# One 1024-column instruction per engine for the split of a weight block, and a ring counted in whole blocks

## The chip, the cores and the metric

The kernel runs on one core of a Trainium2 chip. The metric is the time of one execution in microseconds (us). A profiled execution, taken by the hardware profiler, gives the rows that are read here. TensorE (PE in the profile; PEld is its loading of stationary weights) multiplies matrices, VectorE (DVE) and ScalarE (ACT) work elementwise, GpSimd is POOL, and SyncE (SP) issues the DMA transfers.

## The reference, cut to what matters

The kernel computes an encoder of two layers over 256 tokens of width 1024, in float32. Each layer is

```
h = rms_norm(x);  proj = h @ w_in                      # 50 blocks of 128 output columns
gates = sigmoid(h @ w_gate + b_gate)                   # 24 blocks
o_lru, o_diff, o_swa = mixers(proj)                    # recurrence, two attentions
x += (sum_b gates_b * (o_b @ w_branch_b)) @ w_out      # 24 blocks, then 8 blocks
h = rms_norm(x);  q = h @ w_q                          # 16 blocks
routing weights G from top_k(q @ subkeys)              # 16 experts for each of 8 heads
x += (G * gelu(h @ u.T)) @ v                           # 128 blocks, then 128 blocks
```

A final norm follows. The last product is computed densely: all 16384 experts' activations, weighed by G, which is zero for those that weren't chosen.

## The kernel before

**Blocks.** All weights come from HBM as one stream of blocks of 128 x 1024 float32, 106 blocks for the first part of a layer and 272 for the second, 756 in all. They are of two kinds. In an up block (w_in, w_gate, w_branch, w_q, u) the weights are the stationary operand: 8 pieces of 128 columns, each with three matmuls over 256 tokens, 24 matmuls that add up in one PSUM bank. In a down block (w_out, v) the weights are the moving operand: two halves of 512 columns, two token tiles and three matmuls each, 12 matmuls that add up over all blocks.

**The split.** TensorE multiplies in a shorter format (fp32r), so each operand is split into a high part and the rest, and a product takes three matmuls (hi x hi, hi x lo, lo x hi). For weights, ScalarE writes w_hi (split_hi, L275: a Copy from raw into the fp32r tile) and VectorE writes w_lo = raw - w_hi (split_half, L282). Both work by halves of 512 columns, k = 0 and k = 1; split_lo is the two halves one after the other. For down blocks the activations are split as well: ScalarE a_hi (L366), then VectorE a_lo (L370), each 128x256.

**The ring.** raw holds two pairs of blocks; SyncE loads a pair with one DMA (load_pairs, L259) as soon as the pair that lay there is fully split. w_hi and w_lo hold four halves, which is two blocks. Three semaphores count halves: w_hi_done (ScalarE to VectorE), w_parts (VectorE to TensorE and to SyncE) and w_used (TensorE to ScalarE, one increment behind the last matmul of each half). So ScalarE may write half k of block c when TensorE has used half k of block c-2, and TensorE may start on half k of c when its w_lo is there.

**Order of the work around it.** Each engine runs its own program; in a loop body for up blocks ScalarE does split_hi of block c+1, waits until TensorE has used all of block c, and reads the result of c out of PSUM (L503, L516, L1021, L1042). In the branch blocks VectorE does this reading (L808, L811, L832). In down blocks ScalarE does split_hi and then a_hi, VectorE split_lo and then a_lo, and down_block waits for a_lo of its block as well.

VectorE has other work in many stages: small chains for the recurrence's constants, the convolution, the scan, the lists of top_k. There the halves are put between dependent instructions by hand: half(0), an instruction, half(1), the next, and so on. In the candidate loop (L1176 on), one round handles one list and four U blocks: its last calls are half(5), an is_equal (L1198), half(6), a multiply (L1202), half(7) and a reduction (L1205), the last three over 128x800. The one-hot stage between the up and the down blocks of the second part (L1245 to L1307) uses no weights.

Of the kernel before, what the change touches and what calls it, by code (L numbers as in the profile page):

```python
# [128 lines left out]
def trunk(nc, stream, vecs, cst, rel_bias, bucket_onehot, lam_consts, final_g, diff_lambda, sinks,  # L129
# [6 lines left out]
    with top:  # L136
# [115 lines left out]
        def load_pairs(sp, layer, part_pair, first, end):  # L252

            base = layer * LAYER_PAIRS + part_pair

            def load(p, slot):

                sp.wait_ge(w_parts, p * 4 + 4)
                sp.dma_start(raw[:, slot, :, :], stream[bass.ds(base + p, 1)].rearrange("o b p c -> p (o b) c")).then_inc(raw_in[slot], 16)  # L259
            twos = (end - first) // 2  # L260
            with sp.Fori(0, twos) as n:
                load(n * 2 + first, first % 2)
                load(n * 2 + (first + 1), (first + 1) % 2)
            if (end - first) % 2:
                load(end - 1, (end - 1) % 2)

        def split_hi(act, blk, ring):

            slot, sub = ring // 2, ring % 2
            if sub == 0:  # L270

                act.wait_ge(raw_in[slot], blk * 4 + (16 - 4 * ring))
            for k in range(2):
                act.wait_ge(w_used, blk * 2 + (k + 1))
                act.activation(w_hi[:, (ring % 2) * 2 + k, :], raw[:, slot, sub, 512 * k:512 * k + 512], ACT.Copy).then_inc(w_hi_done, 1)  # L275

        def split_half(dve, blk, ring, k):

            slot, sub = ring // 2, ring % 2
            q = (ring % 2) * 2 + k  # L280
            dve.wait_ge(w_hi_done, blk * 2 + (k + 1))
            dve.tensor_tensor(w_lo[:, q, :], raw[:, slot, sub, 512 * k:512 * k + 512], w_hi[:, q, :].bitcast(F32), ALU.subtract).then_inc(w_parts, 1)  # L282

        def split_lo(dve, blk, ring):

            for k in range(2):
                split_half(dve, blk, ring, k)
# [97 lines left out]
        with nc.Fori(0, DEPTH) as layer:  # L385

            with ExitStack() as part:
# [33 lines left out]
                with nc.Block() as block:  # L421
                    @block.sync
                    def _(sp):
                        sp.sem_inc(w_parts, 8)
# [64 lines left out]
                    def _(act):  # L489
# [24 lines left out]
                        def read_proj(blk, ring):  # L514
                            act.wait_ge(w_used, blk * 2 + 6)
                            act.activation(one(proj[:, bass.ds(blk, 1), :]), bank[ring % 2][:, 0:SEQ], ACT.Copy).then_inc(up_read, 1)  # L516
# [119 lines left out]
                    def _(dve):  # L636
# [165 lines left out]
                        for k in range(16):  # L802
# [3 lines left out]
                            dve.wait_ge(w_used, blk * 2 + 6)  # L806
# [17 lines left out]
                        with dve.Fori(0, 2) as n:  # L824
                            ch.enter(n, 8)
                            for i in range(4):
# [4 lines left out]
                                dve.wait_ge(w_used, blk * 2 + 6)  # L831
# [13 lines left out]
                        add_to_x(dve, bank[2:6], 2 * MIX_BLOCKS + 4)  # L845

                    @block.tensor
                    def _(pe):
                        pe.sem_inc(w_used, 4)
# [113 lines left out]
            with ExitStack() as part:  # L963
# [34 lines left out]
                with nc.Block() as block:  # L998
                    @block.sync
                    def _(sp):  # L1000
                        sp.sem_inc(w_parts, 8)
# [9 lines left out]
                    def _(act):  # L1011
# [5 lines left out]
                        def read_up(dst, func):  # L1017
                            def body(k, blk, ring, n, i):
                                split_hi(act, blk + 1, (ring + 1) % 4)
                                act.wait_ge(w_used, blk * 2 + 6)  # L1020
                                act.activation(one(dst(k)), bank[ring % 2][:, 0:SEQ], func).then_inc(up_read, 1)  # L1021
# [18 lines left out]
                        def read_gelu(k, ring):  # L1040
                            act.wait_ge(w_used, (k + B_U) * 2 + 6)
# [78 lines left out]
                    def _(dve):  # L1120
# [151 lines left out]
                        add_to_x(dve, bank[4:8], 2 * PEER_BLOCKS + 4)  # L1272

                    @block.tensor
                    def _(pe):
                        pe.sem_inc(w_used, 4)
# [132 lines left out]
```

## Time and profile before

| | |
|---|---|
| time, median of 3 runs (lowest to highest) | 2850.52 us (2848.39 to 2858.77) |
| span of the profiled execution | 2819.8 us |
| mean granted TensorE clock | 0.967 |
| TensorE busy | 2601.8 us, 92% |
| VectorE busy | 1788.4 us, 63% |
| ScalarE busy | 1554.7 us, 55% |
| DMA, share of 16 engines | 42.5% |

The span runs from the first to the last instruction of the profiled execution; the time of a run also holds what lies around it. The busy share of TensorE is high because its matmuls overlap in the drawing: each is drawn from its start to its modelled end, and the next starts before that. Distances from start to start show its pace. A wait in a row is the idle time of an engine just before an instruction, with the instruction that ended it.

### The profile page before, as it was taken

What the parts mean: (1) busy time and instruction counts of PE and PEld (TensorE: products, weight loads), DVE (VectorE), ACT (ScalarE), POOL (GpSimd) and SP (SyncE); (2) the same over time, 40 slices, a digit from 0 to 9 for tenths busy, and PEclk for the clock granted to TensorE, in tenths of its full rate; (3) what the DMA queues carried; (4) which work ended last, traced back from release to release, by engine and by line L of the source; (5) the groups of instructions that cost most, each with busy time, mean ns of one, the idle gap of its engine ahead of it and who ended that gap; (6) DMA issues with size and microseconds to landing.
All of it is one profiled execution on the core that took longest, in us unless ns stands there. A gap on an engine that the chain in (4) does not pass through costs nothing. (4 is left out here: it accounts for less than half of the span.)

```text
span 2819.8 us, 57502 instructions
## 1 busy us (share of the span) xinstructions
PE 2601.8 (92%) x17506; PEld 2377.8 (84%) x17506; DVE 1788.4 (63%) x4078; ACT 1554.7 (55%) x3535; POOL 53.4 (2%) x115
## 2 busy tenths in 40 slices
PE   5999999899999769999989999979999997799997
PEld 5998788899999758888779987869999996688886
DVE  3655566377775796666546545654877748966665
ACT  3565344465555785555455643535555558755554
POOL 0000100000000000000000011000000000000000
PEclk9999999899999999999989979989999999999999
DMA  5444123445554205555444431334555541055553
GB/s 181 164 164 156 31 86 135 165 164 179 186 185 164 74 1 193 193 193 193 149 160 164 166 115 28 106 124 163 183 179 186 185 164 45 30 194 193 193 193 141
DMA packets 116256, 413.83 MB, mean 147 GB/s; under 512 B 8104, under 2 KB 18144, under 8 KB 115936
## 3 DMA queue, kind: packets, MB, share of 16 engines
q1 hardware_dynamic: 116192, 413.06, 42.5%
q8 instruction: 30, 0.49, 0.1%
q14 instruction: 34, 0.28, 0.0%
HBM read 411.43 MB, written 4.23 MB: 147 GB/s over the span
## 5 line engine op out<-in xcount | busy, mean ns | idle before, releaser
L282 DVE TENSOR_TENSOR w_lo<-raw,w_hi 128x512 fp32r<-128x512 f32 x1512 | 1023.2, 689 | 751.6 <-ACT w_hi L275 736.3
L275 ACT ACTIVATE w_hi<-raw 128x512 fp32r<-128x512 f32 x1512 | 902.2, 627 | 389.5 <-PE bank L315 307.9
L298 PE MATMUL bank<-h_hi,w_hi 128*128 128x256 f32 x3488 | 998.5, 286 | 28.4 <-DVE w_lo L282 28.4
L299 PE MATMUL bank<-h_lo,w_hi 128*128 128x256 f32 x3488 | 993.0, 285 | 0.0
L300 PE MATMUL bank<-h_hi,w_lo 128*128 128x256 f32 x3488 | 992.6, 285 | 0.0
L298 PEld LDWEIGHTS bank<-h_hi,w_hi 128*128 128x128 f32 x3488 | 675.8, 194 | 33.2 <-DVE w_lo L282 32.9
L299 PEld LDWEIGHTS bank<-h_lo,w_hi 128*128 128x128 f32 x3488 | 676.1, 194 | 0.4
L300 PEld LDWEIGHTS bank<-h_hi,w_lo 128*128 128x128 f32 x3488 | 675.7, 194 | 0.0
L313 PE MATMUL bank<-w_hi,a_hi 128*128 128x512 f32 x1088 | 425.1, 391 | 8.3 <-issue 5.0
L314 PE MATMUL bank<-w_lo,a_hi 128*128 128x512 f32 x1088 | 424.6, 390 | 0.0
L315 PE MATMUL bank<-w_hi,a_lo 128*128 128x512 f32 x1088 | 424.4, 390 | 0.0
L1042 ACT ACTIVATE A<-bank 128x256 f32 (+1 forms) x256 | 98.0, 383 | 341.5 <-PE bank L300 341.5
L313 PEld LDWEIGHTS bank<-w_hi,a_hi 128*128 128x128 f32 x1088 | 205.0, 188 | 51.9 <-issue 5.3
L315 PEld LDWEIGHTS bank<-w_hi,a_lo 128*128 128x128 f32 x1088 | 205.0, 188 | 42.7
L314 PEld LDWEIGHTS bank<-w_lo,a_hi 128*128 128x128 f32 x1088 | 205.1, 189 | 42.3
L1307 PE MATMUL bank<-hot 128*128 128x128 f32 x1024 | 149.0, 289 | 74.7 <-DVE hot L1249 68.7
L1307 PEld LDWEIGHTS bank<-hot 128*128 128x128 f32 x1024 | 125.4, 193 | 98.3 <-issue 85.6
L298 PE MATMUL bank<-o_hi,w_hi 128*128 128x256 f32 x384 | 111.5, 290 | 4.2 <-DVE o_lo L798 4.2
L1099 ACT ACTIVATE hot<-picks,picks_t 128x128 f32<-128x128 f32 x256 | 112.2, 485 | 4.1 <-PE bank L1307 1.7
L299 PE MATMUL bank<-o_lo,w_hi 128*128 128x256 f32 x384 | 110.6, 288 | 0.0
L300 PE MATMUL bank<-o_hi,w_lo 128*128 128x256 f32 x384 | 110.6, 288 | 0.0
L370 DVE TENSOR_TENSOR a_lo<-A,a_hi 128x256 fp32r<-128x256 f32 x256 | 106.8, 417 | 1.0 <-ACT a_hi L366 1.0
(197 smaller groups left out, 2236.7 us busy)
## 6 DMA issues: line engine op xcount, KB each, us to landing
raw<-stream SPq DMA_DIRECT2D x378, 1024.0 KB, 4.8
hank<-rel_hankel SPq DMA_DIRECT2D x16, 256.0 KB, 2.7
rel_hankel<-rel_line SPq DMA_DIRECT2D x1, 3072.0 KB
hank<-rel_hankel SPq DMA_DIRECT2D x16, 128.0 KB, 2.1
A<-subkeys SPq DMA_DIRECT2D x2, 1024.0 KB, 5.0
x<-x_in SPq DMA_DIRECT2D x1, 1024.0 KB, 5.3
qk<-lru_w SPq DMA_DIRECT2D x2, 512.0 KB, 9.1
out<-xr SPq DMA_DIRECT2D x2, 512.0 KB
```

The source lines that it names most:

```text
L275: act.activation(w_hi[:, (ring % 2) * 2 + k, :], raw[:, slot, sub, 512 * k:512 * k + 512], ACT.Copy).then_inc(w_hi_done, 1)
L282: dve.tensor_tensor(w_lo[:, q, :], raw[:, slot, sub, 512 * k:512 * k + 512], w_hi[:, q, :].bitcast(F32), ALU.subtract).then_inc(w_parts, 1)
L298: pe.matmul(ps, hi, rhs_hi(4 * k + c), start=first, stop=False)
L299: pe.matmul(ps, hi, rhs_lo(4 * k + c), start=False, stop=False)
L300: ins = pe.matmul(ps, lo, rhs_hi(4 * k + c), start=False, stop=last)
L313: pe.matmul(ps, hi, w_hi[:, q, :], start=first, stop=False)
L314: pe.matmul(ps, hi, w_lo[:, q, :], start=False, stop=False)
L315: ins = pe.matmul(ps, lo, w_hi[:, q, :], start=False, stop=last)
L370: dve.tensor_tensor(a_lo[:, a, :], src(k), a_hi[:, a, :].bitcast(F32), ALU.subtract).then_inc(a_parts, 1)
L1042: act.activation(one(A[:, bass.ds(k, 1), :]), bank[ring % 2][:, 0:SEQ], ACT.Gelu_apprx_tanh).then_inc(up_read, 1)
L1099: ins = act.activation(hot[:, s, 1, k, :], dist[:, s, k - 1, :], ACT.Relu, scale=picks_t[:, 3, bass.ds(t, 1)], bias=picks_t[:, 2, bass.ds( ...
L1307: ins = pe.matmul(bank[2 + s][:, P * k:P * k + P], hot[:, s, 0, k, :], hot[:, s, 1, k, :], start=True, stop=True)
```

## The change

Each engine splits a whole block with one instruction of 1024 columns. The semaphores w_hi_done, w_parts and w_used count blocks, with starting values of half the former ones, and all waits on them are rewritten. ScalarE waits before the whole block's w_hi until block c-2 is used entirely; TensorE waits once, ahead of a block's first matmul, for the whole w_lo, and increments w_used once, behind its last. split_half keeps its name and its places: with k = 0 it does the whole block, with k = 1 it does nothing. The size of the ring, the loads, the matmuls and all other instructions stay.

```diff
-                sp.wait_ge(w_parts, p * 4 + 4)
+                sp.wait_ge(w_parts, p * 2 + 2)
...
-            for k in range(2):
-                act.wait_ge(w_used, blk * 2 + (k + 1))
-                act.activation(w_hi[:, (ring % 2) * 2 + k, :], raw[:, slot, sub, 512 * k:512 * k + 512], ACT.Copy).then_inc(w_hi_done, 1)
+            act.wait_ge(w_used, blk + 1)
+            act.activation(whole_of(w_hi, ring), raw[:, slot, sub, :], ACT.Copy).then_inc(w_hi_done, 1)
+
+        def whole_of(parts, ring):
+
+            return parts[:, (ring % 2) * 2:(ring % 2) * 2 + 2, :].rearrange("p k c -> p (k c)")
 
         def split_half(dve, blk, ring, k):
 
+            if k:
+                return
             slot, sub = ring // 2, ring % 2
-            q = (ring % 2) * 2 + k
-            dve.wait_ge(w_hi_done, blk * 2 + (k + 1))
-            dve.tensor_tensor(w_lo[:, q, :], raw[:, slot, sub, 512 * k:512 * k + 512], w_hi[:, q, :].bitcast(F32), ALU.subtract).then_inc(w_parts, 1)
+            dve.wait_ge(w_hi_done, blk + 1)
+            dve.tensor_tensor(whole_of(w_lo, ring), raw[:, slot, sub, :], whole_of(w_hi, ring).bitcast(F32), ALU.subtract).then_inc(w_parts, 1)
...
         def up_block(pe, blk, ring, n_up, ps, rhs_hi, rhs_lo):
 
             pe.wait_ge(up_read, n_up + 1)
+            pe.wait_ge(w_parts, blk + 5)
             for k in range(2):
                 q = (ring % 2) * 2 + k
-                pe.wait_ge(w_parts, blk * 2 + (k + 9))
...
-                ins.then_inc(w_used, 1)
+            ins.then_inc(w_used, 1)
...
         def down_block(pe, blk, ring, k_blk, acc, first, last):
 
             pe.wait_ge(a_parts, k_blk + 1)
             a = ring % 2
+            pe.wait_ge(w_parts, blk + 5)
             for k in range(2):
                 q = (ring % 2) * 2 + k
-                pe.wait_ge(w_parts, blk * 2 + (k + 9))
...
-                ins.then_inc(w_used, 1)
+            ins.then_inc(w_used, 1)
...
-                                act.wait_ge(w_used, blk * 2 + 6)
+                                act.wait_ge(w_used, blk + 3)
```

## Rows read from the trace of the kernel before

**Rows 1.** The page's groups: line, engine, operation | busy, mean ns | idle before, releaser

```profile
L282 DVE TENSOR_TENSOR w_lo<-raw,w_hi 128x512 fp32r<-128x512 f32 x1512 | 1023.2, 689 | 751.6 <-ACT w_hi L275 736.3
L275 ACT ACTIVATE w_hi<-raw 128x512 fp32r<-128x512 f32 x1512 | 902.2, 627 | 389.5 <-PE bank L315 307.9
```

**Rows 2.** The waits of the whole span: who <- whom: us in total, times, longest

```profile
DVE w_lo L282 <- ACT w_hi L275: 736.3, 898, 12.1
...
PEld bank L298 <- DVE w_lo L282: 32.9, 17, 4.1
```

**Rows 3.** Windows in up blocks, down blocks, one-hot stage: us, busy (instructions), PEclk, DMA

```profile
575.00:860.00 285.00, 284.55 (x2372) 284.35 (x2371) 222.29 (x652) 153.92 (x373) 0.00 (x0) 1.00 0.52 182
1060.00:1400.00 340.00, 340.00 (x1502) 281.63 (x1501) 214.78 (x375) 195.97 (x374) 0.00 (x0) 1.00 0.55 189
...
1000.00:1040.00 40.00, 26.64 (x185) 22.37 (x186) 40.00 (x95) 35.87 (x95) 0.00 (x0) 1.00 0.00 0
```

**Rows 4.** Timeline in the down blocks: start, us, engine, line, operation [idle <- releaser]

```profile
1201.51 0.39 PE L315 MATMUL bank<-w_hi,a_lo 128*128 128x512 f32 x1
...
1201.93 0.63 ACT L275 ACTIVATE w_hi<-raw 128x512 fp32r<-128x512 f32 x1 [0.73 <-PE bank L315]
...
1202.60 0.69 DVE L282 TENSOR_TENSOR w_lo<-raw,w_hi 128x512 fp32r<-128x512 f32 x1 [0.67 <-ACT w_hi L275]
...
1203.21 0.42 DVE L370 TENSOR_TENSOR a_lo<-A,a_hi 128x256 fp32r<-128x256 f32 x1
...
1204.46 0.39 PE L313 MATMUL bank<-w_hi,a_hi 128*128 128x512 f32 x1
```

**Rows 5.** Timeline in the U blocks, candidate loop

```profile
761.16 0.38 ACT L1042 ACTIVATE A<-bank 128x256 f32 x1 [1.46 <-PE bank L300]
...
761.44 1.14 ACT L275 ACTIVATE w_hi<-raw 128x512 fp32r<-128x512 f32 x2
...
763.62 0.28 PE L300 MATMUL bank<-h_hi,w_lo 128*128 128x256 f32 x1
...
763.74 0.28 PE L298 MATMUL bank<-h_hi,w_hi 128*128 128x256 f32 x1
...
764.22 0.98 DVE L1205 TENSOR_REDUCE A<-A 128x800 f32 x1
```

**Rows 6.** Timeline in the gate blocks

```profile
251.94 1.14 ACT L275 ACTIVATE w_hi<-raw 128x512 fp32r<-128x512 f32 x2
...
254.05 0.28 PE L298 MATMUL bank<-h_hi,w_hi 128*128 128x256 f32 x1
```

**Rows 7.** Longer instructions: ns min/median/max by source line; one group by shape

```profile
L325 ACT ACTIVATE mix<-x x4: 1039/1048/1057, 15.8 to 1416.4; 128x1024 f32<-128x1024 f32 x4
...
L337 ACT ACTIVATE mix<-x,rstd x2: 1149/1150/1151, 19.0 to 1418.6; 128x1024 f32<-128x1024 f32 x2
...
L1343 DVE SCALAR_TENSOR_TENSOR xr<-x,rstd,g_all x2: 1279/1282/1285, 2814.1 to 2815.3; 128x1024 f32<-128x1024 f32 x2
...
L1202 DVE TENSOR_TENSOR A<-A 128x800 f32<-128x800 f32 x32 | 31.5, 984 | 0.0
```

**Rows 8.** Timeline where TensorE stands waiting for a split

```profile
139.44 1.15 ACT L275 ACTIVATE w_hi<-raw 128x512 fp32r<-128x512 f32 x2 [0.20 <-ACT warm L320]
...
140.10 1.29 DVE L282 TENSOR_TENSOR w_lo<-raw,w_hi 128x512 fp32r<-128x512 f32 x2 [4.28 <-ACT w_hi L275]
...
140.85 0.39 PE L298 MATMUL bank<-h_hi,w_hi 128*128 128x256 f32 x1 [0.78 <-DVE w_lo L282]
```

**Rows 9.** Timeline and window after a longer pause of TensorE

```profile
864.38 0.46 PE L298 MATMUL bank<-h_hi,w_hi 128*128 128x256 f32 x1 [2.55 <-DVE w_lo L282]
...
868.86 0.28 PE L298 MATMUL bank<-h_hi,w_hi 128*128 128x256 f32 x1
...
863.00:869.00 6.00, 4.62 (x26) 4.63 (x27) 3.84 (x8) 2.35 (x5) 0.00 (x0) 0.72 0.19 58
```

**Rows 10.** The page's DMA issues: xcount, KB each, median us from issue to landing

```profile
raw<-stream SPq DMA_DIRECT2D x378, 1024.0 KB, 4.8
```

More of the change, by code:

```diff
@@ L272, in split_hi @@
                 act.wait_ge(raw_in[slot], blk * 4 + (16 - 4 * ring))
-            for k in range(2):
-                act.wait_ge(w_used, blk * 2 + (k + 1))
-                act.activation(w_hi[:, (ring % 2) * 2 + k, :], raw[:, slot, sub, 512 * k:512 * k + 512], ACT.Copy).then_inc(w_hi_done, 1)
+            act.wait_ge(w_used, blk + 1)
+            act.activation(whole_of(w_hi, ring), raw[:, slot, sub, :], ACT.Copy).then_inc(w_hi_done, 1)
+        def whole_of(parts, ring):
+            return parts[:, (ring % 2) * 2:(ring % 2) * 2 + 2, :].rearrange("p k c -> p (k c)")
         def split_half(dve, blk, ring, k):
+            if k:
+                return
             slot, sub = ring // 2, ring % 2
-            q = (ring % 2) * 2 + k
-            dve.wait_ge(w_hi_done, blk * 2 + (k + 1))
-            dve.tensor_tensor(w_lo[:, q, :], raw[:, slot, sub, 512 * k:512 * k + 512], w_hi[:, q, :].bitcast(F32), ALU.subtract).then_inc(w_parts, 1)
+            dve.wait_ge(w_hi_done, blk + 1)
+            dve.tensor_tensor(whole_of(w_lo, ring), raw[:, slot, sub, :], whole_of(w_hi, ring).bitcast(F32), ALU.subtract).then_inc(w_parts, 1)
         def split_lo(dve, blk, ring):
-            for k in range(2):
-                split_half(dve, blk, ring, k)
+            split_half(dve, blk, ring, 0)
         def up_block(pe, blk, ring, n_up, ps, rhs_hi, rhs_lo):
             pe.wait_ge(up_read, n_up + 1)
+            pe.wait_ge(w_parts, blk + 5)
             for k in range(2):
                 q = (ring % 2) * 2 + k
-                pe.wait_ge(w_parts, blk * 2 + (k + 9))
                 for c in range(4):
@@ L423, in _ @@
                     def _(sp):
-                        sp.sem_inc(w_parts, 8)
+                        sp.sem_inc(w_parts, 4)
                         sp.dma_start(vec[:], vecs[bass.ds(layer, 1)].rearrange("o p c -> (o p) c")).then_inc(vec_in, 16)
@@ L514, in read_proj @@
                         def read_proj(blk, ring):
-                            act.wait_ge(w_used, blk * 2 + 6)
+                            act.wait_ge(w_used, blk + 3)
                             act.activation(one(proj[:, bass.ds(blk, 1), :]), bank[ring % 2][:, 0:SEQ], ACT.Copy).then_inc(up_read, 1)
@@ L805, in _ @@
                             split_lo(dve, blk + 1, (ring + 1) % 4)
-                            dve.wait_ge(w_used, blk * 2 + 6)
+                            dve.wait_ge(w_used, blk + 3)
                             if k < 8:
@@ L830, in _ @@
                                 split_lo(dve, blk + 1, (ring + 1) % 4)
-                                dve.wait_ge(w_used, blk * 2 + 6)
+                                dve.wait_ge(w_used, blk + 3)
                                 ch(dve.tensor_tensor(gated[:, i % 2, :], one(gates[:, bass.ds(m + 8 * BRANCHES[2], 1), :]), bank[ring % 2][:, 0:SEQ], ALU.mult))
@@ L844, in _ @@
                         blocks_loop(dve, B_OUT, N_OUT - 1, ahead)
-                        add_to_x(dve, bank[2:6], 2 * MIX_BLOCKS + 4)
+                        add_to_x(dve, bank[2:6], MIX_BLOCKS + 2)
                     @block.tensor
                     def _(pe):
-                        pe.sem_inc(w_used, 4)
+                        pe.sem_inc(w_used, 2)
                         pe.sem_inc(up_read, 2)
@@ L1000, in _ @@
                     def _(sp):
-                        sp.sem_inc(w_parts, 8)
+                        sp.sem_inc(w_parts, 4)
                         sp.dma_start(vec[:], vecs[bass.ds(layer, 1)].rearrange("o p c -> (o p) c")).then_inc(vec_in, 16)
@@ L1019, in body @@
                                 split_hi(act, blk + 1, (ring + 1) % 4)
-                                act.wait_ge(w_used, blk * 2 + 6)
+                                act.wait_ge(w_used, blk + 3)
                                 act.activation(one(dst(k)), bank[ring % 2][:, 0:SEQ], func).then_inc(up_read, 1)
@@ L1040, in read_gelu @@
                         def read_gelu(k, ring):
-                            act.wait_ge(w_used, (k + B_U) * 2 + 6)
+                            act.wait_ge(w_used, k + (B_U + 3))
                             act.activation(one(A[:, bass.ds(k, 1), :]), bank[ring % 2][:, 0:SEQ], ACT.Gelu_apprx_tanh).then_inc(up_read, 1)
@@ L1271, in _ @@
                         blocks_loop(dve, B_V, N_V - 1, ahead_v)
-                        add_to_x(dve, bank[4:8], 2 * PEER_BLOCKS + 4)
+                        add_to_x(dve, bank[4:8], PEER_BLOCKS + 2)
                     @block.tensor
                     def _(pe):
-                        pe.sem_inc(w_used, 4)
+                        pe.sem_inc(w_used, 2)
                         pe.sem_inc(up_read, 2)
```

## The prediction, made before the change was run

> **What bounds the kernel now.** I read the page's busy shares first: TensorE is busy for 92% of the span, VectorE for 63%, ScalarE for 55%. The windows say where that is so. In a stretch of the up blocks TensorE is busy for 284.55 of 285 us, in a stretch of the down blocks for 340.00 of 340, both at a granted clock of 1.00, its 2.4 GHz level [rows 3]. The counts there give the pace: an up block of 24 matmuls takes 285 x 24 / 2372 = 2.88 us, a down block of 12 takes 340 x 12 / 1502 = 2.72 us. The reader should see that these stretches leave nothing to gain on TensorE. The change touches no matmul, so a saving on the other two engines is worth something only where TensorE waits for them.
>
> So the next view is the list of waits. TensorE's weight loads waited for a w_lo for 32.9 us in all, in 17 places [rows 2]; that is the most that any faster split can give back. VectorE, in contrast, waits 736.3 us for w_hi [rows 2]: it is idle because ScalarE hands it halves late, not because it has too much to do. The timeline of one block shows the distances that matter, and the rest rests on it.
>
> **The ring.** w_hi and w_lo hold two blocks. Block c may be split only when block c-2 has been used, and must be ready when block c-1 ends. Today this works by halves: the first half of c is written once the first half of c-2 is used, and TensorE starts c on its first half. After the change one ScalarE instruction H writes the whole block once all of c-2 is used, one VectorE instruction L follows it, and TensorE starts only behind both. The two engines no longer overlap on one block, so H + L must fit where half of it did.
>
> **Price of H and L.** No row shows either. Two halves are 2 x 0.689 us on VectorE and 2 x 0.627 us on ScalarE (the L275 row's 902.2 us of busy time over 1512 is less, as pairs overlap) [rows 1]. For H the nearest row is the 128x1024 Square, 1.048 us; the 128x1024 Copy with a scale vector took 1.150 and is my upper bound [rows 7]. I take 1.05, since the split has no scale vector. For L the 128x800 two-input operation took 0.984 us against 0.689 for 512 columns, 1.02 ns a column, so 1024 columns come to 1.21 to 1.22; the 128x1024 instruction with two inputs and a scalar, 1.282, is the upper bound [rows 1, 7]. I take 1.22. The lower bound for H + L is 2.20, a little below either slope; the upper is 2.43; I use 2.27. The Trainium skill (VectorE: DVE Perf Modes, the section on the TRN2 errata) gives (N+151)/0.96 ns for an fp32 two-input operation and 224 + N cycles of 1.2 GHz for ScalarE. By that L would be 1.22 and H 1.04, an estimate; the 512-column rows agree with it within 0.02 us, and the sum would be about 2 us lower.
>
> **Down blocks (2 x 134 that follow two others).** The last matmul of c-2 starts at 1201.51, the w_hi that waits for it at 1201.93. Then come w_lo at 1202.60, a_lo at 1203.21 (0.08 before that w_lo ends, 0.42 long), and the first matmul of block c at 1204.46 [rows 4]. The second half's chain thus ends at 1203.63, 0.83 us ahead of need. With the change: 1201.93 + 1.05 = 1202.98; + 0.04 to VectorE's start (1202.56 to 1202.60 today); + 1.22 = 1204.24; a_lo 0.08 earlier, 0.42 long: 1204.58; + 0.05 until a waiting TensorE starts (a w_lo that starts at 140.10 and lasts 0.69 releases a matmul at 140.85 [rows 8]) = 1204.63. That is 0.17 us late. A matmul that had to wait also refills the pipe: the one at 140.85 is drawn with 0.39 us where the others have 0.28 [rows 5, 8], so I add 0.10. As the chain runs from c-2 to c, this 0.27 us is paid once for two blocks: 0.135 a block, 268 x 0.135 = 36 us. Bounds: 0.05 a block (H + L at 2.20, no refill) and 0.215.
>
> **Up blocks that ScalarE reads out plainly.** The read of bank starts at 761.16, w_hi at 761.44, and the next-but-one block's first matmul at 763.74 [rows 5]. With the change 761.44 + 1.05 + 0.04 + 1.22 + 0.05 = 763.80, late by 0.06; with the refill 0.16 for two blocks, 0.08 a block. ScalarE's order doesn't change here: it reads block c-2's bank, for which it waits until all of c-2 is done, before it splits c. So its new wait costs nothing of itself, and only the missing overlap does. This holds for 110 blocks of a layer (46 of the first ones and of the query projection, 64 of the U matrix): 220 x 0.08 = 18 us. Bounds 0 and 0.16 a block.
>
> **The candidate loop (16 rounds of 4 U blocks in each layer).** VectorE's other work stands between the splits, and a k = 1 call now does nothing, so its half moves up to the k = 0 call. Behind a round's last split stand the multiply and the reduction of 0.98 us each (the reduction is the one at 764.22) [rows 5, 7], which nothing separates any more: they take 0.90 + 0.05 for the wait on the product + 0.89, and the next split may start 1.84 us after the last one ended. With 1.22 + 0.05 this is 3.06 us from block start to block start where 2.88 are wanted. With refills and the ring's chain that makes about 0.4 us a round, 32 rounds: 13 us. Bounds 0 and 22.
>
> **Gate blocks (23 in each layer).** The bias read is longer, so w_hi starts later: 251.94, for a matmul at 254.05 [rows 6]. 251.94 + 2.36 = 254.30, late by 0.25, with refill 0.35 for two: 0.175 x 46 = 8 us. Bounds 4 and 12.
>
> **Cold starts.** Where TensorE already stands waiting for a split, it waits for H and L instead of two halves: w_hi at 139.44, matmul at 140.85, 1.41 us [rows 8]; with the change 2.36, so 0.95 more. There are 17 such waits [rows 2]: 16 us. Bounds 15 and 19.
>
> **At nothing.** The convolution blocks have two more fp32 matmuls between each two blocks, which cover the lateness; without that cover they would pay as the plain ones. The branch blocks are bound by VectorE's own read-out, beside which H is hidden; there the last block of a run may pay some tenths. SyncE's load waits for the odd block's w_lo, as before, with nothing else queued behind it but the next load. From the end of L to the next use of that slot lie three blocks less H + L, at least 3 x 2.72 - 2.31 = 5.85 us, against 4.8 us to landing [rows 10]. The saved instructions, 756 on each engine, and their semaphore increments give nothing: both engines wait most of the time.
>
> **The sum.** 36 + 18 + 13 + 8 + 16 = 91 us. The profiled span is 2819.8 us; the median of the runs, 2850.5, has 30.7 us around it, which the change doesn't touch. So 2911 for the span and 2942 for the time. Lower bounds: 13 + 0 + 0 + 4 + 15 = 32, 2882. Upper bounds: 58 + 35 + 22 + 12 + 19 = 146, 2997.
>
> **A rule for and one against.** VectorE is idle for over a third of the span and its idle time before w_lo is ScalarE's lateness [rows 1, 2]; TensorE is the full engine [rows 3]. By the rows, then, shorter total work on the two buys nothing and a longer path from use to ready costs. The Trainium skill has a rule for the change (Advanced Engine Details and Errata, TRN2 Errata: tiles of 512 or 1024 elements, so that the latency between instructions is paid less often) and one against it (Perfetto Trace Analysis, Optimizing Scalar/DVE Operations: "If Scalar/Vector aren't saturated, but are causing bubbles on other engines, breaking up instructions may allow work to be completed sooner"). By the first the kernel would be no slower; by the second, slower; the trace so far bears out the second.
>
> **Rivals.** (1) The forecast, 2942: the whole-block chain is longer than two blocks of TensorE's work nearly everywhere. Chance 0.84 for 2882 to 3010.
> (2) The pauses also cost clock. One wait of 2.55 us, at 864.38, was followed by a granted clock of 0.72 over those 6 us, with matmuls at the 1.2 GHz level, and by a block that took until 868.86, 4.48 us instead of 2.88 [rows 9]. Were that to befall one block in eight of the 662 that are late, 83 x 1.6 = 133 us would come on top: 3075. Against it: in the one-hot stage TensorE is busy for 26.64 of 40 us in short turns and holds 1.00 [rows 3], and my pauses are 0.2 to 0.3 us. Chance 0.07. The Trainium skill (TensorE: Matmul & The Clock Gate) likewise has the throttle as the default and activity as what releases it; the one-hot row decides that this much idleness is borne.
> (3) The chain just fits: H + L comes out under 2.10, VectorE and ScalarE overlap more at their edges than drawn, and only the 17 cold starts pay: 2850.5 + 16 = 2866 at most, or the lower bounds' 2882. For it speaks that the up blocks miss by only 0.06 us. Against it, that the down blocks would need 0.17 us less, more than the rows of 1024 columns allow. Chance 0.08, a third of it within 0.5% of before.
> (4) Faster: VectorE's queue, not the chain, makes TensorE wait in the 17 places, and the merged instruction, about 0.16 us shorter than two, clears it sooner. It decides where VectorE has no idle time ahead of w_lo; the most that it gives is all 32.9 us [rows 2], 2818. At the cold start the opposite is seen: w_lo follows w_hi at once after VectorE was idle [rows 8]. Chance 0.01.
>
> **The numbers.** Time 2942. The range for 8 in 10 takes the bounds of the unknown costs: 2885 to 3010. A measurement can tell about 0.5% of this kernel from no change; faster by more than that 0.01, within 0.03, slower by more 0.96.
>
> **What would show it.** In the profile after: w_hi at 1.05 and w_lo at 1.22 us, 756 of each; in the down stretch matmul blocks 2.85 us apart instead of 2.72, with a_lo (not w_lo) as what TensorE waits for; in the up stretch pauses of less than 0.2 us that w_lo ends; the granted clock still 1.00 in both; 17 cold starts longer by 0.95. Wrong it would be if TensorE stays at full busy time in the down stretch, or if H + L is off 2.27 by a tenth: each tenth of a microsecond is 0.05 a block, 33 us.

## The result

The changed kernel is slower. In the first comparison its median is 2926.4 us (2920.0 to 2934.2, four runs) against 2849.5 us (2847.2 to 2858.8), a ratio of 1.034 (95% interval 1.0245 to 1.0435). In a second one it is 2938.9 us (six runs) against 2839.2 us (seventeen), 1.0445 (1.0368 to 1.0522). The forecast was 2942 us, in a range of 2885 to 3010. Medians are over all runs; the ratios leave out the executions that took over 1.5% longer than the fastest of the same kernel.

The page of the kernel after, its groups (line, engine, operation, shapes, count | busy, mean ns of one | idle before, releaser):

```profile
L286 DVE TENSOR_TENSOR w_lo<-raw,w_hi 128x1024 fp32r<-128x1024 f32 x756 | 925.8, 1225 | 919.6 <-ACT w_hi L274 917.1
...
L274 ACT ACTIVATE w_hi<-raw 128x1024 fp32r<-128x1024 f32 x756 | 798.6, 1057 | 499.3 <-PE bank L318 415.8
```

L is 1.225 us and H 1.057, where 1.22 and 1.05 were forecast. VectorE has 97 us less to do with the splits than in [rows 1], ScalarE 104 us less, and VectorE waits 181 us longer for w_hi. The saved time has become waiting (the loads are not what is waited for: ScalarE waited for raw for 17.1 us before and for 0.7 us after). TensorE waits as well, as the list of waits of the kernel after shows (who <- whom: us in total, times, longest), against 32.9 us in 17 places in [rows 2]:

```profile
PEld bank L301 <- DVE w_lo L286: 68.3, 102, 5.0
PEld bank L316 <- DVE w_lo L286: 60.5, 124, 0.5
```

Windows of the kernel after in the U blocks and the down blocks, with the columns of [rows 3]:

```profile
700.00:850.00 150.00, 149.52 (x1205) 145.60 (x1204) 110.38 (x202) 70.40 (x126) 0.00 (x0) 1.00 0.51 175
1130.00:1400.00 270.00, 266.85 (x1112) 201.11 (x1111) 144.74 (x186) 126.36 (x185) 0.00 (x0) 1.00 0.52 181
```

The busy time of TensorE hardly shows it, since matmuls are drawn up to their modelled ends; the counts do. An up block takes 150 x 24 / 1205 = 2.99 us instead of 2.88, a down block 270 x 12 / 1112 = 2.91 instead of 2.72. The granted clock is 1.00 in both.

**Where the time went.** Between two marks that both traces have (the first matmul of the blocks named, in the timelines), in us, both layers together:

| stage | before | after | more | forecast |
|---|---|---|---|---|
| blocks 0 to 50 | 324.1 | 340.4 | 16 | 15 |
| gate blocks 51 to 72 | 130.7 | 139.2 | 8 | 8 |
| attention stage | 256.8 | 245.4 | -11 | 0 |
| 24 branch blocks | 156.4 | 152.5 | -4 | 0 |
| output blocks and the norm behind them | 83.6 | 88.0 | 4 | 2 |
| query, U, one-hot stage | 1089.9 | 1121.8 | 32 | 32 |
| 128 down blocks, first matmul to last | 697.0 | 748.1 | 51 | 34 |

The forecasts here are the prediction's terms dealt out by stage. The attention stage, in which no line of the change stands, has moved by 11 us, and that had to be understood before the medians could be. The 4 us of the branch blocks come with the clock as well, and aren't shown to be a gain: the granted clock there was 0.95 before and 1.00 after, and in a second profile of the kernel after, at 0.98, the same blocks took 155.6 us.

**The attention stage is a matter of the single execution.** The windows of the attention stages of four kernels: before (both layers), then one layer each of three that are described below (whole-block counters with halves between the engines; two instructions without overlap; the dense burst). All run the same instructions there but for the burst of the last:

```profile
266.00:389.00 123.00, 115.24 (x646) 86.34 (x646) 61.71 (x221) 52.65 (x216) 24.20 (x53) 0.91 0.11 32
1656.00:1789.00 133.00, 125.81 (x653) 94.37 (x651) 62.03 (x221) 52.67 (x216) 24.37 (x53) 0.82 0.11 31
```

```profile
1678.00:1843.00 165.00, 156.94 (x649) 118.05 (x647) 62.05 (x221) 52.39 (x216) 23.75 (x53) 0.63 0.08 24
```

```profile
285.00:441.00 156.00, 147.31 (x654) 110.47 (x653) 62.35 (x222) 52.49 (x216) 23.57 (x53) 0.68 0.09 27
```

```profile
266.00:387.00 121.00, 113.16 (x688) 87.04 (x686) 61.65 (x221) 52.60 (x216) 23.75 (x53) 0.97 0.11 33
```

The first count in brackets is that of TensorE's matmuls, about 650 each time (688 with the burst); the third figure from the end is the granted clock. The same work takes 123 us a layer at 0.91, 156 at 0.68 and 165 at 0.63; with the burst, whose 7 us are included, it is 121 at 0.97. Over the twelve profiles of this study the two stages together take from 242 to 321 us. Each run lists its time, span and mean granted clock; of 17 executions of the kernel before in one comparison, these three show the relation:

```
time 2801.1 us, clock 0.976
time 2847.2 us, clock 0.954
time 2876.5 us, clock 0.944
```

The time outside this stage (the span less both attention stages) is what the change can be read from. It was 2563.0 us before, 2672.8 and 2673.5 us in two profiles of the kernel after: 110 us more, 3.9% of the span. This measure itself scatters by a few us, as the branch blocks show: in the profile of the kernel before with the dense burst (described below) it is 2559.6. The first comparison of the medians showed less, 77 us. If the rest of the kernel is taken as constant, the median execution of the kernel before had some 285 us in the attention stage there and that of the kernel after some 252; this is inferred from the times, since only one execution of each comparison was profiled.

### The profile page after: what moved, and what is told of

It is laid out like the page before. It is cut to its first block and busy times, and to the rows that moved or that the text cites. A ratio compares the mean times of both kernels' runs of the same rounds, so it can differ in the third digit from the quotient of the medians.

```text
span 2918.2 us, 53872 instructions
## 1 busy us (share of the span) xinstructions
PE 2671.7 (92%) x17506; PEld 2361.0 (81%) x17506; DVE 1725.6 (59%) x3322; ACT 1451.8 (50%) x2779; POOL 53.6 (2%) x115
## 5 line engine op out<-in xcount | busy, mean ns | idle before, releaser
L286 DVE TENSOR_TENSOR w_lo<-raw,w_hi 128x1024 fp32r<-128x1024 f32 x756 | 925.8, 1225 | 919.6 <-ACT w_hi L274 917.1
L301 PE MATMUL bank<-h_hi,w_hi 128*128 128x256 f32 x3488 | 1021.2, 293 | 46.5 <-DVE w_lo L286 43.2
L274 ACT ACTIVATE w_hi<-raw 128x1024 fp32r<-128x1024 f32 x756 | 798.6, 1057 | 499.3 <-PE bank L318 415.8
L316 PE MATMUL bank<-w_hi,a_hi 128*128 128x512 f32 x1088 | 442.3, 407 | 17.6 <-issue 5.0
```

Of the source, the lines that this page charges most:

```text
L274: act.activation(whole_of(w_hi, ring), raw[:, slot, sub, :], ACT.Copy).then_inc(w_hi_done, 1)
L286: dve.tensor_tensor(whole_of(w_lo, ring), raw[:, slot, sub, :], whole_of(w_hi, ring).bitcast(F32), ALU.subtract).then_inc(w_parts, 1)
```

## The experiments

**The changed kernel once more.**

> The changed kernel again, unchanged, beside five more runs of the one before. The profiles so far show that outside the attention stage the changed kernel takes 108.5 us more (2612.9 against 2504.4 us), while the attention stage, on which the change has no line, took 252 to 317 us in five kernels, with granted clocks there of 0.53 to 0.96. If that stage is a matter of the single execution, the profile shows 105 to 112 us more outside it once more, and the times differ by that much give or take 30 us. If the change itself speeds the attention stage, that stage takes 255 us or less again.

Measured: 2938.9 us (2931.3 to 2966.8), 1.0445 as above; outside the attention stage 110.5 us more than before, and this time 266 us within it. So nothing shows that the change speeds that stage; its time comes with the execution. (The two totals in the expectation leave out some 59 us more than those used here, in both kernels alike; their difference, 108.5, stands for the 110 here.)

All "outside" figures below are spans less the attention stages, from the profile of the kernel named; the base is 2563.0 us.

**Whole-block counters, but halves between the engines.** From the kernel after:

```diff
-            act.activation(whole_of(w_hi, ring), raw[:, slot, sub, :], ACT.Copy).then_inc(w_hi_done, 1)
+            for k in range(2):
+                act.activation(w_hi[:, (ring % 2) * 2 + k, :], raw[:, slot, sub, 512 * k:512 * k + 512], ACT.Copy).then_inc(w_hi_done, 1)
...
-            dve.wait_ge(w_hi_done, blk + 1)
-            dve.tensor_tensor(whole_of(w_lo, ring), raw[:, slot, sub, :], whole_of(w_hi, ring).bitcast(F32), ALU.subtract).then_inc(w_parts, 1)
+            for k in range(2):
+                q = (ring % 2) * 2 + k
+                dve.wait_ge(w_hi_done, blk * 2 + (k + 1))
+                ins = dve.tensor_tensor(w_lo[:, q, :], raw[:, slot, sub, 512 * k:512 * k + 512], w_hi[:, q, :].bitcast(F32), ALU.subtract)
+            ins.then_inc(w_parts, 1)
```

> From the changed kernel: whole-block counters for TensorE and for ScalarE's wait stay, but each engine again works in two 512-column instructions and hands over by halves. From w_hi's start to a whole block being ready it takes 0.67 + 1.29 + 0.05 = 2.01 us instead of 2.36. Theory (the lost overlap inside a block): the down blocks are 0.35 us per two blocks better off and come back to 2.72 to 2.75 us, plain up blocks to 2.88; what remains is 17 cold starts of 0.6 us (10 us) and some 0.09 a block where VectorE has long work between splits (11 us): 2865 to 2885 us. Rival A (counting whole blocks is itself what costs, since TensorE frees and gets a block later): as the changed kernel, about 2926.

Measured: 2880.7 us (2877.2 to 2893.9), ratio to before 1.0126 (1.0034 to 1.0218); outside 2583.6 us, 21 more than before and 89 less than after. The windows of this kernel:

```profile
700.00:850.00 150.00, 150.00 (x1235) 148.59 (x1235) 115.53 (x254) 77.27 (x182) 0.00 (x0) 1.00 0.53 182
1130.00:1400.00 270.00, 270.00 (x1182) 215.86 (x1181) 159.89 (x295) 143.48 (x295) 0.00 (x0) 1.00 0.55 192
```

2.92 and 2.74 us a block. TensorE still waits for whole blocks and still frees them whole, yet four fifths of the cost are gone. So it is not the counting that costs most (rival A). What this kernel has back is that VectorE works on the first half while ScalarE does the second, but its instructions are short again too; the next experiment tells the two apart.

**Two instructions each, without overlap.** From the kernel after; w_hi_done and w_parts are incremented behind the second of two 512-column instructions:

```diff
+            for k in range(2):
+                ins = act.activation(w_hi[:, (ring % 2) * 2 + k, :], raw[:, slot, sub, 512 * k:512 * k + 512], ACT.Copy)
+            ins.then_inc(w_hi_done, 1)
...
+            dve.wait_ge(w_hi_done, blk + 1)
+            for k in range(2):
+                q = (ring % 2) * 2 + k
+                ins = dve.tensor_tensor(w_lo[:, q, :], raw[:, slot, sub, 512 * k:512 * k + 512], w_hi[:, q, :].bitcast(F32), ALU.subtract)
+            ins.then_inc(w_parts, 1)
```

> From the changed kernel: all counters stay whole, also between ScalarE and VectorE, but each engine uses two 512-column instructions. The whole block is ready 1.15 + 0.04 + 1.29 + 0.05 = 2.53 us after w_hi starts, 0.17 more than in the changed kernel. Theory (length of the chain over the ring): 0.085 us a late block more, 662 blocks, so 2926 + 56 + 3 = 2985 us. Rival B (the long instruction as such costs, by holding its engine or by reading memory beside TensorE): faster than the changed kernel, towards 2850 to 2900.

Measured: 3035.8 us (3028.7 to 3043.0), 1.0662 (1.0566 to 1.0758). Of that the attention stages have 311 us (the row at 0.68 above is this kernel's); outside 2729.4 us, 56.6 more than after, where 59 were forecast. Its windows:

```profile
700.00:850.00 150.00, 147.24 (x1177) 142.27 (x1176) 111.26 (x293) 75.01 (x181) 0.00 (x0) 1.00 0.51 171
1130.00:1400.00 270.00, 257.91 (x1080) 194.65 (x1080) 148.26 (x276) 130.21 (x269) 0.00 (x0) 1.00 0.50 169
```

3.06 and 3.00 us a block. Rival B has fallen: the long instructions as such cost nothing; in the place that the change gives them they are even better than two short ones. With short instructions in both kernels, handing over halves or not makes 146 us (2583.6 against 2729.4). The chain's length sets the pace.

**ScalarE's half of the change alone.** From the kernel before:

```diff
-            for k in range(2):
-                act.wait_ge(w_used, blk * 2 + (k + 1))
-                act.activation(w_hi[:, (ring % 2) * 2 + k, :], raw[:, slot, sub, 512 * k:512 * k + 512], ACT.Copy).then_inc(w_hi_done, 1)
+            q = (ring % 2) * 2
+            act.wait_ge(w_used, blk * 2 + 2)
+            act.activation(w_hi[:, q:q + 2, :].rearrange("p k c -> p (k c)"), raw[:, slot, sub, :], ACT.Copy).then_inc(w_hi_done, 2)
```

> From the kernel before: only ScalarE's half of the change, one 1024-column w_hi that waits for the whole of block c-2; VectorE and TensorE keep halves. Theory: up blocks start on the first half, which is ready 1.05 + 0.04 + 0.69 + 0.05 = 1.83 us after w_hi starts, where 2.30 are free, so they stay at 2.88; down blocks wait for a_lo behind both halves, 0.07 us later than in the changed kernel, 0.235 a block over their 2.72: 63 us; cold starts 0.43 x 17 = 7 us. 2849 + 70 = 2919 us, nearly all of it in the down blocks. Rival A (whole counters): half of the changed kernel's cost in every stage, about 2888.

Measured: 2914.8 us (2884.9 to 2939.9), 1.0145 (0.9998 to 1.0292); outside 2636.5 us, 73.5 more than before (70 forecast). Its windows:

```profile
700.00:850.00 150.00, 149.97 (x1250) 149.77 (x1249) 111.44 (x264) 73.81 (x131) 0.00 (x0) 1.00 0.53 182
1130.00:1400.00 270.00, 261.71 (x1086) 196.84 (x1085) 146.65 (x270) 123.47 (x181) 0.00 (x0) 1.00 0.52 175
```

Up blocks keep 2.88 us, down blocks take 2.98: nearly the whole cost, 68 us in the 128 down blocks of both layers, lies where a_lo must follow both halves.

**VectorE's half alone.** From the kernel before, one w_lo of 1024 columns at the k = 0 call:

```diff
+            if k:
+                return
...
-            dve.wait_ge(w_hi_done, blk * 2 + (k + 1))
-            dve.tensor_tensor(w_lo[:, q, :], raw[:, slot, sub, 512 * k:512 * k + 512], w_hi[:, q, :].bitcast(F32), ALU.subtract).then_inc(w_parts, 1)
+            dve.wait_ge(w_hi_done, blk * 2 + 2)
+            dve.tensor_tensor(whole(w_lo), raw[:, slot, sub, :], whole(w_hi).bitcast(F32), ALU.subtract).then_inc(w_parts, 2)
```

> From the kernel before: only VectorE's half of the change, one 1024-column w_lo behind both halves of w_hi; ScalarE keeps halves and half counters. Theory: in the down blocks ScalarE's first half again runs ahead, the chain is 0.42 us shorter than in the changed kernel, and they come back to 2.72 us; in up blocks both halves of w_hi start together behind the read of the bank, so the block is ready 1.15 + 0.04 + 1.22 + 0.05 = 2.46 us after w_hi starts, 0.10 later than in the changed kernel: 0.13 a plain block (27 us), 0.16 in the U blocks with lists (20), 0.22 a gate block (10), 18 of cold starts. 75 us outside the attention stage, all of it in up blocks. Rival A (whole counters for TensorE's start are what costs): down blocks late as well, by half of the changed kernel's 0.2.

Measured: 2983.5 us (2943.4 to 2988.9), 1.0499 (1.0378 to 1.062), with 321 us of attention in the profile; outside 2662.4 us, 99 more than before, where 75 were forecast. Its windows:

```profile
700.00:850.00 150.00, 147.10 (x1179) 142.29 (x1178) 108.31 (x244) 74.15 (x176) 0.00 (x0) 1.00 0.49 172
1130.00:1400.00 270.00, 268.31 (x1175) 213.82 (x1174) 152.69 (x197) 153.75 (x294) 0.00 (x0) 1.00 0.54 187
```

The pattern is as forecast, the mirror image of the one before: up blocks at 3.05 us, worse than in the kernel after (ScalarE's two halves take longer than its one whole), down blocks nearly back, at 2.76. The sizes were too low, 75 us where 99 were measured: 0.18 us a block in the candidate loop instead of 0.16, 0.04 a down block where I had put nothing (8 us), and more in the first stage. Neither half of the change is harmless; each spoils one kind of block.

**Four pieces instead of two.** From the kernel before, each half by two instructions of 256 columns, counters as they were:

```diff
+                for j in range(2):
+                    ins = act.activation(w_hi[:, (ring % 2) * 2 + k, 256 * j:256 * j + 256], raw[:, slot, sub, 512 * k + 256 * j:512 * k + 256 * j + 256], ACT.Copy)
+                ins.then_inc(w_hi_done, 1)
...
+            for j in range(2):
+                c = slice(256 * j, 256 * j + 256)
+                ins = dve.tensor_tensor(w_lo[:, q, c], raw[:, slot, sub, 512 * k + 256 * j:512 * k + 256 * j + 256], w_hi[:, q, c].bitcast(F32), ALU.subtract)
+            ins.then_inc(w_parts, 1)
```

> From the kernel before: each half is split by two instructions of 256 columns on each engine, 3024 on each instead of 1512; the counters stay at halves. Theory (only the path from use to ready counts, and it has 0.3 us to spare where each half gets 0.1 us longer): within 5 us of before outside the attention stage, with more busy time on both engines. Rival D (instruction count and fixed cost per instruction limit this kernel): about as much slower as the saving that the merge was to bring, 100 us or more.

Measured: 2842.0 us (2807.8 to 2857.9) beside 2839.2 of before; outside 2564.4 us, 1.4 more. Its windows:

```profile
700.00:850.00 150.00, 150.00 (x1253) 150.00 (x1252) 119.73 (x366) 87.71 (x286) 0.00 (x0) 1.00 0.54 182
1130.00:1400.00 270.00, 270.00 (x1193) 223.64 (x1192) 184.10 (x496) 174.46 (x496) 0.00 (x0) 1.00 0.55 192
```

In the down stretch VectorE has 496 instructions where the kernel before has 297 and the kernel after 186, and TensorE doesn't notice. Rival D has fallen: twice the instructions cost 1.4 us, no more than the measure scatters, so their number, which the change cuts, is no limit of this kernel. In the Trainium skill's terms (Perfetto Trace Analysis, Optimizing Scalar/DVE Operations) grouping is for a saturated engine and breaking up for one that causes bubbles on others; the experiment with whole-block counters and this one agree with that, by the 89 us that handing over halves gives back and the 1.4 us that twice the instructions cost.

**A ring of four blocks for the down blocks.** From the kernel after. In the 128 down blocks of each layer's second part the idle tiles h_hi and h_lo hold two more blocks; ScalarE waits for block c-4 ahead of w_hi and for c-2 only ahead of a_hi:

```diff
-            act.wait_ge(w_used, blk + 1)
-            act.activation(whole_of(w_hi, ring), raw[:, slot, sub, :], ACT.Copy).then_inc(w_hi_done, 1)
+            act.wait_ge(w_used, blk - 1 if deep else blk + 1)
+            act.activation(whole_of(w_hi, ring, deep), raw[:, slot, sub, :], ACT.Copy).then_inc(w_hi_done, 1)
+
+        def held(parts, ring, deep):
+
+            if deep and ring >= 2:
+                spare = h_hi if parts is w_hi else h_lo
+                return spare[:].rearrange("p a s -> p (a s)").rearrange("p (k c) -> p k c", c=512)
+            return parts
...
-                            split_hi(act, blk + 1, (ring + 1) % 4)
+                            split_hi(act, blk + 1, (ring + 1) % 4, True)
+                            act.wait_ge(w_used, blk + 2)
                             part_hi(act, src, k + 1, (ring + 1) % 2)
```

> From the changed kernel: in the 128 down blocks of each layer's second part the ring of w_hi and w_lo holds four blocks (the tiles of h_hi and h_lo, idle there, take the other two); the instructions stay 1024 columns long and the counters whole, and ScalarE waits for block c-2 only ahead of a_hi, whose ring stays at two. Theory (the chain over a ring of two): those blocks come back to 2.72 us, 51 us less than the changed kernel: 2875 us; the up blocks stay late. Rival C (what delays TensorE there is its own restart behind two semaphores, or the loads): they stay at 2.85 or more, 2926.

Measured: 2912.8 us (2882.4 to 2914.6), 1.0205 (1.0096 to 1.0314); outside 2624.7 us, 48 less than after (51 forecast). The median lies above the forecast by the attention stage, of which the profiled execution, the fastest of the four, had little. Its window in the down blocks:

```profile
1130.00:1400.00 270.00, 270.00 (x1193) 223.58 (x1192) 164.01 (x199) 138.30 (x198) 0.00 (x0) 1.00 0.57 194
```

1193 matmuls, exactly as before, with the long instructions and the whole counters in place. The 128 blocks of both layers take 697.0 us as in the kernel before. In these blocks the cost is the chain measured against the depth of the ring, and nothing else. Rival C has fallen. A deeper ring for the up blocks wasn't tried; they stay late, at 3.00 us in the candidate loop.

**A dense burst ahead of the attention stage.** From the kernel before, to take away the scatter:

```diff
                         pe.wait_ge(lru_sig, DC + 2)
+                        pe.wait_ge(up_read, 2 + B_BR)
+                        pe.wait_ge(staged, 1)
+                        for j in range(40):
+                            pe.matmul(bank[j % 2][:, 0:SEQ], h_hi[:, j % 8, 0:P], h_hi[:, j % 8, :], start=True, stop=True)
```

> From the kernel before: 40 more matmuls of fp32r 128x256 in each layer, ahead of the attention stage's first scores, into banks that nobody reads; they are work for nothing. In the profiles the attention stage starts at the lower clock level and stays there for 20 to 100 us, and this differs between executions. If a dense burst brings the clock up and it stays up, the attention stage takes 120 to 125 us a layer every time, burst included 128: some 30 us less than the median of before, and less spread. If the stage's own thin matmuls let the clock fall again, 5 to 9 us a layer are lost: 2860 to 2870.

Measured: 2802.6 us, 2797.1 to 2804.7 in twelve runs, where before spreads from 2801.1 to 2876.5; ratio 0.9918 (0.9888 to 0.9948). Both attention stages take 121.3 us, the burst included, and the granted clock is 0.97 there (its row is shown with the attention windows above). Ahead of the burst TensorE had stood idle for 0.91 us and done thin transposes; its row in this kernel's timeline:

```profile
271.86 7.41 PE L887 MATMUL bank<-h_hi 128*128 128x256 f32 x40 [0.91 <-POOL qk L471]
```

40 matmuls in 7.4 us are 0.19 apart on average, where 0.12 is the pace at the 2.4 GHz level; the distances from start to start are 0.21 us or more for the first 25 and 0.12 for the last 14. So it starts at the lower level and ends at the upper one, and the stage then keeps it. This kernel beats both others, at the price of 80 matmuls that compute nothing.

**The change on that base.** The kernel after with the same burst:

> The changed kernel with the same dense burst ahead of the attention stage. That takes the attention stage's scatter out of the comparison: against the 2802.6 us of the kernel before with the burst, the change alone should show its cost outside that stage, 108 to 110 us by two profiles: 2912 us, within 2905 to 2920, and a spread of 10 us or less. If the change were to act on the attention stage as well, the difference would be another.

Measured: 2920.1 us (2914.8 to 2922.3), at the upper edge of what was expected; outside 2671.0 us, 108 more than before, and 121.2 and 120.8 us of attention. The difference to 2802.6 is 117 us by medians that come from two comparisons, 111 us by the two profiled executions, and the two have 242.6 and 242.0 us of attention. With the scatter gone, the change costs 4%. Against the kernel before without the burst, measured in the same comparison (2846.4 us), the ratio is 1.0255 (1.0212 to 1.0298), as the burst's gain is in it.

**TensorE's two waits change places.** On top of the last one:

```diff
-            pe.wait_ge(a_parts, k_blk + 1)
-            a = ring % 2
-            pe.wait_ge(w_parts, blk + 5)
+            pe.wait_ge(w_parts, blk + 5)
+            a = ring % 2
+            pe.wait_ge(a_parts, k_blk + 1)
```

> The same as e8, and TensorE's two waits ahead of a down block change places: first for w_lo, which comes early, then for a_lo, which comes last. The changed kernel's profile has 0.12 us from the end of a_lo to the first weight load of the next block, where a single wait took 0.05. If the second wait's handling behind the late one is what makes it 0.12, the load comes 0.06 us sooner, 0.03 us a down block, 8 us in all: 2904 us. If 0.12 is simply what a late a_lo costs, it stays at 2912 and the down blocks at 2.92 us.

Measured: 2910.5 us (2904.8 to 2912.4), 9.5 less, and no execution of the one reaches the other's range; the 256 down blocks take 740.2 us instead of 747.6. Its timeline:

```profile
1133.02 0.42 DVE L373 TENSOR_TENSOR a_lo<-A,a_hi 128x256 fp32r<-128x256 f32 x1
...
1133.49 0.19 PEld L316 LDWEIGHTS bank<-w_hi,a_hi 128*128 128x128 f32 x1 [0.43 <-DVE a_lo L373]
```

a_lo ends at 1133.44, the load follows after 0.05 us. This holds for all 126 late blocks of the two layers (every second one): 0.05 us from the end of a_lo to the load, where the kernel without the swap has 0.12 in all of its 126.

## Why the prediction was right, and where it wasn't

**The down blocks: the mechanism right, the term too small.** The timeline of the kernel after, at a place that answers to [rows 4]:

```profile
1130.84 0.39 PE L318 MATMUL bank<-w_hi,a_lo 128*128 128x512 f32 x1
...
1131.27 1.06 ACT L274 ACTIVATE w_hi<-raw 128x1024 fp32r<-128x1024 f32 x1 [1.39 <-PE bank L318]
1131.29 0.19 PEld L316 LDWEIGHTS bank<-w_hi,a_hi 128*128 128x128 f32 x1 [0.49 <-DVE w_lo L286]
1131.30 0.49 PE L316 MATMUL bank<-w_hi,a_hi 128*128 128x512 f32 x1
...
1132.36 1.23 DVE L286 TENSOR_TENSOR w_lo<-raw,w_hi 128x1024 fp32r<-128x1024 f32 x1 [1.19 <-ACT w_hi L274]
...
1133.51 0.42 DVE L373 TENSOR_TENSOR a_lo<-A,a_hi 128x256 fp32r<-128x256 f32 x1
...
1134.05 0.19 PEld L316 LDWEIGHTS bank<-w_hi,a_hi 128*128 128x128 f32 x1 [0.17 <-issue]
1134.15 0.40 PE L316 MATMUL bank<-w_hi,a_hi 128*128 128x512 f32 x1
```

Step by step: 0.43 to w_hi, 1.06, 0.03, 1.23, a_lo 0.08 before its end, 0.42. All that is as worked out. a_lo ends at 1133.93, but the load starts only at 1134.05, 0.12 later, not 0.05, and its matmul 0.10 behind it. From the last matmul of c-2 to the first of c it is 3.31 us where my step gave 3.12 (1201.51 to 1204.63), and 3.21 for the block that shows the wait, every second one. I had taken the 0.05 from a place with one wait, while a down block has two in a row and the late one comes first. The swapped waits give the 0.07 back, worth 7 us in the down blocks: shown. The rest is mainly the restart, which I had put at 0.10 from up blocks: a down block that had to wait takes 0.13 us longer from its first matmul to its last (2.62 us, from 1131.30 on, instead of 2.49). Two blocks take 5.84 us instead of 5.44, 0.20 a block where 0.135 was forecast, and the term is 51 us in the 128 down blocks of a layer's second part and 2 in the output blocks, not 36. The lines' releasers also mislead here: the waits name w_lo, as the row at 1131.29 does, and "issue" at 1134.05. By the ends a_lo is the last in both, as forecast, and with the waits in the other order the row itself says so.

**Up blocks.** The timeline of the kernel after, against [rows 5]:

```profile
737.87 1.06 ACT L274 ACTIVATE w_hi<-raw 128x1024 fp32r<-128x1024 f32 x1
...
738.15 0.99 DVE L1208 TENSOR_REDUCE A<-A 128x800 f32 x1 [0.15 <-DVE A L1205]
739.06 1.22 DVE L286 TENSOR_TENSOR w_lo<-raw,w_hi 128x1024 fp32r<-128x1024 f32 x1
...
740.33 0.39 PE L301 MATMUL bank<-h_hi,w_hi 128*128 128x256 f32 x1
```

This is the candidate loop's place that was named: w_hi is ready at 738.93, but the reduction holds VectorE until 739.06, and the block starts 0.05 after w_lo. The 56 blocks that lie wholly inside the loop take 6.3 us a layer more, 0.11 each, where about 0.10 was forecast. (The prediction wrote this block's length as 1.84 + 1.22 + 0.05 = 3.06; that sum is 3.11, and from one w_lo's end to the next only the first two terms count, 3.06. The longest block of a round measured 3.08.) The plain blocks ahead of the gates run at 2.97 us (+0.09, forecast 0.08), the gate blocks at 3.05 (+0.17, forecast 0.175); another 1 us of that stage's 8 comes from the clock in its first block. The convolution blocks keep their time, 3.55 and 3.05 us in turn, as forecast.

**Cold starts.** At the place of [rows 8] w_hi now starts at 144.73 and the matmul at 147.11, 2.38 us (2.36 forecast). Not every cold start paid that much: at the place of [rows 9] TensorE's idle time grew from 2.55 to 2.96 us only. One thing came on top. This window follows it:

```profile
146.00:152.00 6.00, 4.89 (x28) 4.90 (x29) 2.95 (x4) 2.45 (x6) 0.00 (x0) 0.72 0.56 175
```

TensorE's idle time ahead of the matmul grew from 0.78 to 1.72 us, the clock fell, and the block behind it took 4.46 us. That is the second rival's mechanism, at this place in both layers, 1.5 us each. It isn't bound to the place: in the second profile of the kernel after, the same idle time of 1.72 us is followed by a block of 2.97 us, and the clock falls behind 1.8 us at block 9 instead, where it had held at 1.00 in the first. It did not spread to the late blocks: in the windows of the up and down blocks above the clock stays at 1.00.

**The base of the sum was wrong.** I took the 30.7 us between the profiled span and the median for time around the span. In every execution listed, time and span are 1.8 us apart. The profiled execution was simply a quick one, 2821.6 us, with 257 us of attention; a median one, 29 us longer, has some 286, by the same inference. The mean clock beside the span could have raised the question. This left the forecast of the time as it was, since it starts from the median; it made the span's 2911 a forecast for a quick execution, where 2918.2 was measured. The forecast for the change itself, 91 us, was 19 too low against 110. With 110 on the median of 2850 the time would have been 2960; it was 2926 because the kernel after had quick executions in the first comparison. That 2942 lies within 0.6% of it is therefore partly luck: the error of the terms and the luck of the clock went opposite ways.

**The rivals.** The third (the chain just fits) fell with H and L. The fourth (a shorter stay in VectorE's queue makes it faster) fell with the result: w_lo became 0.15 us shorter than two, and TensorE waited longer at the cold starts. The quarters add that more instructions in that queue don't slow the kernel either, 1.4 us for twice as many. The Trainium skill's rule for larger tiles (Advanced Engine Details and Errata, TRN2 Errata) is true of the engines here, 1.225 us for one against 2 x 0.689, but by it the kernel would have been no slower, and it is 110 us slower: the rule says nothing about the kernel's time.

## What to carry to other kernels

Two engines in series on one buffer ring must be judged by the path from "slot free" to "slot ready" against the ring's depth times the consumer's pace, not by their busy time. Merging pieces shortens each engine's work and lengthens this path by what used to overlap. If long instructions are wanted, first find more slots: with a ring of four they cost nothing in the down blocks. And before medians are compared, split the spans by stage: a stage that the change doesn't touch can move more than the one that it does.

## What the runs showed of the hardware that I had not expected

- The granted clock of a stage of thin matmuls (attention) differs between executions that run the same instructions: 123 us a layer at 0.91, 133 at 0.82, 156 at 0.68, 165 at 0.63. A burst of 40 dense matmuls ahead of it pinned it at 0.97 in both layers and took the scatter of twelve runs down to 8 us, at a gain of 0.8%. The Trainium skill (TensorE: Matmul & The Clock Gate, What's actually happening) has activity as what releases the throttle; this agrees. Why the thin matmuls, at a busy share of over 90% in the drawing, leave it undecided is open.
- Two semaphore waits in a row on TensorE, with the late one first, cost 0.12 us from the end of the late instruction to the weight load; with the late one last, 0.05 us.
- A block whose first matmul had to wait takes longer from its first matmul to its last: 0.09 us in up blocks (128x256; 2.85 instead of 2.76) and 0.13 us in down blocks (128x512; 2.62 instead of 2.49).
